# Three closing projections, the stages behind them and the end in halves of the tokens, with no barrier between

## The reference

```python
def second_block(x, ...):
    pos = jnp.arange(x.shape[1], dtype=jnp.int32)
    for layer in range(DEPTH):                                   # 2
        h = rmsnorm(x, norm_mix_pre[layer])
        if layer < N_A_LAYERS:
            m = retention_mixer(h, ...)                          # ends with 2048 -> 1024
        else:
            m = dilated_mixer(h, ..., k_sh, v_sh, pos)           # ends with 1024 -> 1024
        x = x + rmsnorm(m, norm_mix_post[layer])
        f = conv_ffn(rmsnorm(x, norm_ffn_pre[layer]), ...)       # ends with 2816 -> 1024
        x = x + rmsnorm(f, norm_ffn_post[layer])
        if layer == N_A_LAYERS - 1:
            k_sh, v_sh = shared_kv(x, kv_norm, att_w_kv, pos)
    return x

def rmsnorm(x, g):
    y = x * lax.rsqrt(jnp.mean(x * x, axis=-1, keepdims=True) + RMS_EPS)
    return y * g
```

## Time and profile before

| what | value |
|---|---|
| three runs | 2992.29, 2993.57, 2996.12 us |
| median | 2993.57 us |
| profiled execution, first to last instruction | 2993.2 us |
| instructions | 39031 |
| TensorE busy | 2953.5 us, 99% |
| TensorE weight loads | 2355.3 us, 79% |
| VectorE busy | 1719.4 us, 57% |
| ScalarE busy | 1049.0 us, 35% |
| GpSimd busy | 1279.0 us, 43% |
| mean granted clock of TensorE | 0.993 of 2.4 GHz |

### The profile page before, as it was taken

One profiled execution on the slowest core, in us unless ns is written; L12 is line 12 of the kernel. 1 busy time (PEld: TensorE's weight loads), 2 busy tenths in 40 slices (PEclk: granted clock), 3 DMA queues, 4 the chain that ended last, 5 costly groups with the idle time before them and its releaser, 6 DMA issues.

```text
span 2993.2 us, 39031 instructions
## 1 busy us (share of the span) xinstructions
PE 2953.5 (99%) x15224; PEld 2355.3 (79%) x15224; DVE 1719.4 (57%) x3004; ACT 1049.0 (35%) x1863; POOL 1279.0 (43%) x926
## 2 busy tenths in 40 slices
PE   8999999999999999999999999999999999999999
PEld 6777778887777778777778788887888888788887
DVE  4765455475745555735553587615766666587721
ACT  4443343354443432533322322224333333432221
POOL 3333334453333345544444455544434434355543
PEclk9999999999999999999999999999999999999999
DMA  5222223232222223232222233322222222223332
GB/s 194 81 78 67 71 78 96 85 113 71 78 64 71 78 85 99 85 106 78 85 85 79 83 99 95 98 96 95 78 78 71 78 78 78 71 88 96 99 99 71
DMA packets 78331, 260.22 MB, mean 87 GB/s; under 512 B 10730, under 2 KB 13546, under 8 KB 78148
## 3 DMA queue, kind: packets, MB, share of 16 engines
q1 hardware_dynamic: 77572, 255.63, 26.9%
q10 hardware_dynamic: 576, 2.10, 0.2%
HBM read 255.53 MB, written 6.09 MB: 87 GB/s over the span
## 4 chain that ended last, share of the span: by engine, by line
PE 93%; DVE 3%; ACT 1%; DMA 1%; issue 1%; POOL 0%; SPq 0%; PEldq 0%; DVEq 0%; ACTq 0%; PEld 0%
PE bank L707 25%; PE bank L709 24%; PE bank L708 24%; PE bank L845 2%; PE bank L892 2%; PE bank L872 1%; PE bank L724 1%; PE bank L1059 1%; PE bank L725 1%; PE bank L731 1%; PE bank L1009 1%; PE bank L1010 1%; PE bank L1015 1%; PE bank L1095 1%; PE bank L761 1%
## 5 line engine op out<-in xcount | busy, mean ns | idle before, releaser
L558 POOL TENSOR_TENSOR w_lo<-w_raw,w_hi 128x512 fp32r<-128x512 f32 x458 | 610.8, 1334 | 1630.9 <-ACT w_hi L1234 1630.9
L707 PE MATMUL bank<-h_hi,w_hi 128*128 128x512 f32 x2367 | 944.9, 399 | 0.5 <-POOL w_lo L558 0.5
L709 PE MATMUL bank<-h_hi,w_lo 128*128 128x512 f32 x2367 | 924.4, 391 | 0.0
L708 PE MATMUL bank<-h_lo,w_hi 128*128 128x512 f32 x2367 | 923.0, 390 | 0.0
L1234 ACT CAST w_hi<-w_raw 128x1024 fp32r<-128x1024 f32 x458 | 479.9, 1050 | 1259.4 <-PE bank L709 1164.2
L560 POOL TENSOR_TENSOR w_lo<-w_raw,w_hi 128x512 fp32r<-128x512 f32 x458 | 665.1, 1452 | 36.0
L707 PEld LDWEIGHTS bank<-h_hi,w_hi 128*128 128x128 f32 x2367 | 445.5, 188 | 97.4 <-issue 8.8
L709 PEld LDWEIGHTS bank<-h_hi,w_lo 128*128 128x128 f32 x2367 | 444.9, 188 | 95.8
L708 PEld LDWEIGHTS bank<-h_lo,w_hi 128*128 128x128 f32 x2367 | 446.1, 188 | 86.4 <-issue 0.3
L2107 DVE TENSOR_SCALAR m<-bank,gains 128x512 f32<-128x512 f32 x48 | 36.0, 751 | 328.6 <-ACT ta L1437 197.0
L1372 ACT ACTIVATE probs<-probs,small_columns 128x128 f32<-128x128 f32 (+2 forms) x192 | 101.9, 531 | 168.3 <-DVE small_columns L1866 164.1
(11 more groups left out here) (311 smaller groups left out, 4411.9 us busy)
## 6 DMA issues: line engine op xcount, KB each, us to landing
w_raw<-in_w SPq DMA_DIRECT2D x458, 512.0 KB, 3.5
bias_copies<-bias_vectors SPq DMA_DIRECT2D x1, 2560.0 KB
x_res<-in_x_t ACTq DMA_DIRECT2D x4, 512.0 KB, 8.3
bias<-bias_copies SPq DMA_DIRECT2D x8, 256.0 KB, 3.3
bias<-bias_copies SPq DMA_DIRECT2D x16, 128.0 KB, 2.4
out_x<-x_res SPq DMA_DIRECT2D x8, 256.0 KB, 2.9
bias_copies<-bias_vectors SPq DMA_DIRECT2D x1, 1280.0 KB
ple_raw<-in_p_t SPq DMA_DIRECT2D x2, 512.0 KB, 3.6
```

What stands on the lines that cost most here:

```text
L558: pool.tensor_tensor(WL[slot][:, 0:half], RAW[slot][:, 0:half], WH[slot][:, 0:half].bitcast(F32), ALU.subtract).then_inc(sems["lo_half"], 1)
L707: pe.matmul(banks[bank][:], WH[slot][:, w], hi[:, k, :], start=start, stop=False)
L708: pe.matmul(banks[bank][:], WH[slot][:, w], lo[:, k, :], start=False, stop=False)
L709: pe.matmul(banks[bank][:], WL[slot][:, w], hi[:, k, :], start=False, stop=stop).then_inc(sems["kt_done"], 1)
```

## The change

The last tile of `linear` in ret and ffn, and the last two in dil, are multiplied in two halves of 256 tokens: all steps for the first half, then all steps for the second half with the same weights, in another bank. Each half has its own sums, variance, root, reciprocal and two transposes. The next stages ffn0, dil, ffn1 and end have no barrier before them. Their first three tiles are multiplied in halves too: all k for half 0, then all k for half 1. DVE and ACT make x, `h_hi` and `h_lo` by halves, with separate operations. In dil the two operands change places (HH and H2H), and all eight `kv_hi` come behind both halves. At the end, half 0 is scaled, added and stored before half 1. The core of the diff, with new functions in full:

```diff
+HALF_ROW = SEQ // 2
+HALVES = (slice(0, HALF_ROW), slice(HALF_ROW, SEQ))
+IN_HALVES = {"post": 0, "ret": 1, "ffn": 1, "dil": 2}
...
 # SP
-            sp.wait_ge(sems["x_ready"], 4 * KT)
+            sp.wait_ge(sems["x_ready"], 6 * KT)
...
+            for k in range(KT):
+                sp.wait_ge(sems["x_ready"], 8 * KT + k + 1)
+                sp.dma_start(out[:, k, HALVES[0]], X[:, k, HALVES[0]]).then_inc(sems["stored"], t.add("stored", 16))
...
 # POOL
-            pool.wait_ge(sems["x_ready"], 4 * KT)
+            pool.wait_ge(sems["x_ready"], 6 * KT)
...
+        BEHIND_HALF = ("ffn0", "dil", "ffn1", "end")
...
-                if e.stage > 1 and name not in BEHIND_PLE:
+                if e.stage > 1 and name not in BEHIND_PLE and name not in BEHIND_HALF:
                     e.begin_stage()
...
 # PE
+                def half_tile(self, bank, hi, lo, k, start, stop, h, name=None):
+                    slot, w, c = self.n // SLOT % RING, slice(self.n % SLOT * P, (self.n % SLOT + 1) * P), HALVES[h]
+                    self.weights_in()
+                    pe.matmul(banks[bank][:, c], WH[slot][:, w], hi[:, k, c], start=start, stop=False)
+                    pe.matmul(banks[bank][:, c], WH[slot][:, w], lo[:, k, c], start=False, stop=False)
+                    ins = pe.matmul(banks[bank][:, c], WL[slot][:, w], hi[:, k, c], start=False, stop=stop)
...
+                def later_sums(self, name):
+                    split = IN_HALVES[name]
+                    t.up("m_squared", split)
+                    pe.wait_ge(sems["m_squared"], t.at("m_squared"))
+                    self.half_sums(name, [TC, TA, TB] if split == 2 else [TC, TB], 1, True, True).then_inc(sems["summed"], t.one("summed"))
+                def fresh_halves(self, opened, hi, lo, half, name):
...
+                    for h in range(2):
+                        self.n = base
+                        for k in range(KT):
...
+                            pe.wait_ge(sems["operand_hi"], t.at("operand_hi", behind))
...
+                            for bank in opened:
...
+                                pe.matmul(half(banks[bank][:], h), WH[slot][:, w], half(hi[:, k, :], h), start=(k == 0), stop=False)
+                                pe.matmul(half(banks[bank][:], h), WL[slot][:, w], half(hi[:, k, :], h), start=False, stop=False)
...
+                            pe.wait_ge(sems["operand"], t.at("operand", behind))
...
+                                ins = pe.matmul(half(banks[bank][:], h), WH[slot][:, w], half(lo[:, k, :], h), start=False, stop=(k == KT - 1))
+                                if h == 1:
+                                    ins.then_inc(sems["kt_done"], 1)
+                            if (h, k) == (0, 0):
+                                self.later_sums(name)
+                            elif (h, k) == (0, 3):
+                                self.half_spread(name, 1)
...
 # PE, linear
-                    for _ in range(first, KT):
+                    split = IN_HALVES[name]
+                    for _ in range(first, KT - split):
...
+                    if split:
+                        opened, n = [self.rotate() for _ in range(split)], self.n
+                        for bank in opened:
+                            for k in range(nk):
+                                self.half_tile(bank, hi, lo, k, k == 0, k == nk - 1, 0, "half_done" if k == nk - 1 else None)
+                        self.n = n
+                        pe.wait_ge(sems["evicted"], self.tiles - split)
+                        self.half_sums(name, [TC], 0, True, False)
+                        for at_ in range(split):
...
+                            for k in range(nk):
+                                self.half_tile(bank, hi, lo, k, k == 0, k == nk - 1, 1, "kt_done")
+                                if (at_, k) == (0, 0):
...
+                                    self.half_sums(name, [TA, TB] if split == 2 else [TB], 0, False, True).then_inc(sems["summed"], t.one("summed"))
+                                elif (at_, k) == (0, 4):
+                                    self.half_spread(name, 0)
+                        return
...
 # ACT
+                def operand_halves(self, name, dst, g, half_of_x, half, sq, squared):
+                    half_root(0)
+                    for h in range(2):
+                        for k in range(KT):
+                            t.up("x_ready")
+                            act.wait_ge(sems["x_ready"], t.at("x_ready"))
+                            act.activation(half(dst[:, k, :], h), half_of_x(X[:, k, :], h), ACT.Copy, scale=gain(g, k)).then_inc(sems["operand_hi"], t.one("operand_hi"))
+                            if h:
+                                act.activation(sq[:, k, :], X[:, k, :], ACT.Square).then_inc(sems[squared], t.one(squared))
+                            elif k == 0:
+                                hi(self.n - 2 * SLOT)
+                            elif k == 2:
+                                hi(self.n - SLOT)
+                            elif k == 4:
+                                self.squares(name, 1)
+                                hi(self.n)
+                            elif k == 6:
+                                half_root(1)
...
 # ACT, dilated
-                    self.postnorm(M2)
+                    self.operand_halves("ffn", HH, "mixpre1", by_class_half, in_class_half, SQD, "dil_squared")
                     for k in range(KT):
-                        t.up("x_ready")
-                        act.wait_ge(sems["x_ready"], t.at("x_ready"))
-                        act.activation(in_class(H2H[:, k, :]), by_class(X[:, k, :]), ACT.Copy, scale=gain("mixpre1", k)).then_inc(sems["operand_hi"], t.one("operand_hi"))
-                        act.activation(SQD[:, k, :], X[:, k, :], ACT.Square).then_inc(sems["dil_squared"], t.one("dil_squared"))
-                        for j in ((k // 2,) if k % 2 else ()) + (tuple(range(KT // 2, KT)) if k == KT - 1 else ()):
-                            act.activation(in_class(HH[:, j, :]), by_class(X[:, j, :]), ACT.Copy, scale=gain("kv", j)).then_inc(sems["kv_hi"], t.one("kv_hi"))
+                        act.activation(in_class(H2H[:, k, :]), by_class(X[:, k, :]), ACT.Copy, scale=gain("kv", k)).then_inc(sems["kv_hi"], t.one("kv_hi"))
                     t.up("cleared", 6)
                     self.past(3, KT)
...
 # DVE
+                def postnorm_halves(self, name, l, g, half_of_x, half):
...
+                    half_variance(name, 0)
+                    half_inverse(0)
+                    for h in range(2):
+                        t.up("rstd_spread")
+                        dve.wait_ge(sems["rstd_spread"], t.at("rstd_spread"))
+                        if h:
+                            dve.wait_ge(sems["evicted"], self.tiles)
+                        scaled(0, h)
+                        added(0, h)
+                        for k in range(KT):
+                            if k + 1 < KT:
+                                scaled(k + 1, h)
+                            dve.wait_ge(sems["x_ready"], t.at("x_ready"))
+                            t.up("operand_hi")
+                            dve.wait_ge(sems["operand_hi"], t.at("operand_hi"))
+                            dve.scalar_tensor_tensor(half(HL[:, k, :], h), half_of_x(X[:, k, :], h), gain(g, k),
+                                                     half(HH[:, k, :].bitcast(F32), h), ALU.mult, ALU.subtract).then_inc(sems["operand"], t.one("operand"))
+                            if k + 1 < KT:
+                                added(k + 1, h)
+                            if (h, k) == (0, 5):
+                                half_variance(name, 1)
+                        if h == 0:
+                            half_inverse(1)
+                            self.second_half(name, l)
```

More of the change, by code:

```diff
@@ new lines, in half_sums @@
+                def half_sums(self, name, squares, h, first, last):
+                    for a, sq in enumerate(squares):
+                        for b in (2 * h, 2 * h + 1):
+                            ins = pe.matmul(banks[sums_bank(name, h)][:, b:b + 1], sq[:, b * P:(b + 1) * P], ONES[:, 0:1],
+                                            start=(first and a == 0 and b == 2 * h),
+                                            stop=(last and a == len(squares) - 1 and b == 2 * h + 1), skip_group_check=True)
+                    return ins
@@ L967, in close @@
                         pe.wait_ge(sems["scaled"], t.at("scaled"))
-                        pe.matmul(banks[CLOSE_BANKS[k]][:], ID[:], M2[:, k, :], start=False, stop=True).then_inc(sems["added"], t.one("added"))
+                        pe.matmul(banks[CLOSE_BANKS[k]][:, c], ID[:], M2[:, k, c], start=False, stop=True).then_inc(sems["added"], t.one("added"))
                     self.tiles -= BY_PE
@@ L986, in ffn_up @@
                 def ffn_up(self, l):
-                    self.spread(OUTB)
```

(39 more changed lines are left out.)

155 lines of the change are left out of this document (103 added, 52 removed).

## The result

The changed kernel takes 3009.4 us (median of 4 runs, 3007.97 to 3010.22) against 2994.47 for the kernel before in the same comparison: 1.0047 of its time, 95% interval 1.0034 to 1.0059. Forecast were 3007.8 us and "slower" with 0.66. The profiled execution has a span of 3008.1 us, 14.9 more than before's 2993.2.

What follows compares the result with a forecast made beforehand. TensorE, busy 99% of 2993.2 us, was taken as the bound. Terms of -0.1 + 5.5 + 0.5 + 9.4 + 1.7 - 2.8 = +14.2 us gave 3007.8 us, range 2999.5 to 3019, down to 2993.5 for A.

Steps and rivals of the forecast that it cites:

- Step (1): Closing tiles and next stages' first tiles: a half matmul costs 0.120 us, or 0.113 if cost goes by column.
- Step (2): New stages' first tiles: the DVE and ACT cycle per half k takes 1.47 us, 1.91 in class order.
- Step (3): Next stages' starts, without POOL and clock: -0.1 us behind retention, +0.5 behind the dilated stage, +5.5 before kv.
- POOL terms: First-half chains: seven weight chunks, each lengthening DVE's operations by 1.34 us while POOL makes its low part.
- The kv order: Dilated stage's start: eight kv high parts, 9.0 us, precede the next weights' cast; TensorE waits over 3 us; loss 5.5.
- Step (4): First-half chains: POOL's low parts of seven chunks hold DVE for 9.4 us in all; bounds nothing and 15.4.
- Step (5): TensorE's cold clock after waits: hidden at the first k, 1.7 us lost before kv; bounds 0 and 10.
- Step (6): End of the kernel: the span ends 29.2 us after the last tile's start against 32.0, a gain of 2.8.
- A: First-half chains: half operations slip between POOL's, so no hold; 2996.7 us, no measurable change; chance 0.16.
- C: Before kv: a late TensorE hides the kv high parts, +5.5 us falls to 1, total 3003; within the chain's 0.66.
- B: Seams: TensorE sets the end and the halves hide the norm, -20.2 us, 2973.4 in all; chance 0.13.
- D: Chains: TensorE stays at 1.2 GHz, each chain lengthens by up to 7 us, 3021 or more; chance 0.05.

Runs made afterwards that it cites:

- e2: Changed kernel with DVE adding x two k ahead of the low part instead of one behind it: 2991.6 us, 0.9988 of the kernel before.
- e4: Changed kernel with the second half's sums behind the first half's k = 4, not 0, and spread behind k = 7, not 3: 3013.39 us, 1.0057.
- e3: Changed kernel with next weights cast behind the fourth kv high part, not the eighth, and three chunks loaded before SP waits for x: 3007.59 us, 1.0037.
- e9: e7 plus e3's cast and loads, and the kv reciprocal moved behind the last kv low part: 2988.05 us, 0.9974 of the kernel before.
- e7: e2 with the second half's sums behind the first half's k = 2 and its spread behind k = 7: 2990.62 us, 0.9983.
- e5: Changed kernel with GpSimd making only 64 of 1024 columns of seven chunks' low parts in the first-half chains: 3003.44 us, 1.0032.
- e6: Changed kernel with halves only in ffn 1's closing tile and the close, the other three seams as before: 2991.61 us, 0.9990.

## Why the prediction was right, step by step

**Step (1), half matmuls.** In the closing tiles they start 0.120 us apart (48 in 5.75 us), the price taken.

**Step (2), the half cycle.** 1.47 us forecast and 1.47 measured; 1.91 and 1.89 to 1.94 in class order. That this chain, and not TensorE, sets the end is shown by e2: with the wait for ACT out of the cycle it falls to 1.06 and each seam of this form shortens by 4.4 to 5.5 us, though the halves, their fixed cost and TensorE's work stay as they are.

**Step (3), the early start.** DVE's first scaling starts at S + 8.85 behind retention (9.0 forecast). N was S + 36.7, with two of the seven POOL terms of 1.34 S + 39.4; measured S + 40.4. The last `added` is at S + 36.3 where step (3) with POOL's part says 35.4: POOL's part is 0.7 longer than taken, and from the eighth `added` to the next half's first it is 3.0 us where 2.7 was counted, of which DVE stands 0.55 for the second spread. Behind the dilated stage 40.5 was forecast with POOL's part and 42.5 measured: POOL's part is 1.0 longer, and the stretch between the halves is 4.3 us. There TensorE sums squares of two tiles at half clock and the spread comes later. The prediction had the cold clock hidden at the first k; here it cost 1.0 to 1.2 us by this spread. e4 shows it by an edit, and e3, whose program is the same at this seam, by chance: its clock was low for a shorter time, the spread went out at S + 26.1 instead of 27.2, and N is 1.0 earlier. The stretches around the cold clock, first in the changed kernel, then in e3:

```profile
2624.40:2635.50 11.10, 8.35 (x39) 8.35 (x40) 8.18 (x16) 3.50 (x8) 3.92 (x3) 0.54 0.29 96
2623.40:2630.60 7.20, 5.50 (x26) 5.50 (x27) 5.79 (x11) 3.08 (x8) 2.88 (x3) 0.56 0.35 102
```

For kv, S + 54.4, with three POOL terms 58.4 and with the clock 60.1, against 57.7 measured to the start: the 1.7 us of clock were not lost there, and 3 x 1.34 was 0.6 too much.

**The kv order.** Eight kv high parts in a row take 9.03 us (9.0 forecast), and TensorE then waits 3.5 us on `w_lo`. e3 shows that the cast's place is the cause of the late start, and that moving the cast alone gains 0.75 us at the end of the kv matmuls. With the reciprocal moved as well it is 5.9 (e9 against e7), of which 2.5 are a clock that stayed up; the reciprocal was not moved alone.

**Step (4), POOL.** The mechanism was right, and the size nearly so. In the first half behind retention the two chunks lengthen the chain by 3.4 us (13.7 for 7 x 1.47 = 10.3), 1.7 each where 1.34 was taken; behind ffn 0 three chunks lengthen it by 3.4 (16.75 for 7 x 1.91), 1.1 each, and behind the dilated stage two by 3.7 (13.97). That makes 10.5 us on the chain, 9.4 forecast. e5 takes 10.0 of them away (3.3, 3.4 and 3.3), and the starts behind come 1.6, 3.4 and 3.8 us earlier, 8.8 in all; what is missing is DVE's wait for the second spread behind retention. That the marks gained only 5.6 is the clock's doing.

**Step (5), the clock.** Forecast 1.7 us, lost before kv. It was not lost there: the kv matmuls ran at 1.00 and took 11.0 us. Instead 1.7 us were lost behind N of retention, where TensorE's wait of 1.8 us for the first weights was followed by 3.4 us at a granted clock of 0.51 (1.2 GHz): from N to the sums it is 9.9 us for 8.2. Right size, wrong place, by luck: in e4 and e5 such stretches stand at two more places, 1.6 us each. And the cold clock at the first k, put at nothing, cost 1.0 to 1.2 us behind the dilated stage, as said under step (3).

**Step (6), the close.** The gain was 4.1 us, 2.8 forecast. DVE's last `added` starts at S + 24.4 and ends at 24.8, where 25.2 was forecast, and the end follows 3.1 us behind, for the 4.0 taken: the span ends at S + 27.9 instead of 29.2. e6 shows that the gain stands alone.

**The sum.** By seams: forecast +2.6, +3.2 and +11.2 us (retention, dilated, ffn 0 with the clock) and -2.8, measured +5.4, +5.1, +8.4 and -4.1. The total of 14.9 against 14.2 is closer than its terms: two were 2 to 3 us short, one 3 us long, and the close 1.3 short of its gain. The mechanism held, but that the sum fell within 1 us is luck.

**The rivals.** A, no hold by POOL, gave 2996.7; with the hold taken out (e5) the kernel is still at 3003.4. The starts are near step (3): N at S + 38.8 and 38.7 for 36.7 and 37.8, kv at 54.3 for 54.4. What A leaves out is the clock, some 5 us in e5 (1.8, 1.6 and 1.6), and the wait for the second spread behind retention. C, a kv order that hurts less, is out: without the hold the kv matmuls still start over 5 us later than before the change. B, halves that hide the norm, named 1.08 us as the cycle from which it decides. e2 and e7 reach 1.06. The sign then turns, to 0.9988 and 0.9983, but most of B's 5.5 us at a seam stays out: S to N behind retention is 35.0 us in e7, with a clock of 1.00 and TensorE busy for 32.0 of them, not 31.3. What is left is mainly TensorE's wait for the second half's first high part, 1.5, and one for the next weights, 1.2. D, a clock that stays down in the chain, is refuted: it is 1.00 in e4 over the whole chain.

## What to carry to other kernels

Halving a step's width halves neither DVE's nor ACT's part of it; before a producer chain that hands each tile from DVE to ACT and back is cut finer, work out its cycle with the waits in it and compare it with the consumer's, and give DVE one or two tiles of lead in its queue, which here was worth as much as the whole change cost. Where a stage is made to start earlier, look at what is cast, loaded or inverted in the same queues at that time: here the second spread, the kv reciprocal and the sums of the squares each became the next wait as soon as the one ahead of it was gone. Price each seam by itself, from its first matmul to a common mark; four seams of opposite sign hid behind one total.

## What the runs showed of the hardware that was not expected

After a wait of 1.8 to 3.5 us TensorE's granted clock did not always fall, and the length of the wait does not tell. Behind the wait of 1.8 us before N behind retention it was 0.51 (1.2 GHz) for 3.4 us. Behind a wait of 1.8 us before N behind the dilated stage it stayed at 1.00 in the same execution, and fell in e3, e4 and e5 (36 matmuls in 9.9 us for 8.3). The 48 kv matmuls behind a wait of 3.5 us ran at 1.00 in the changed kernel (11.0 us) and at 0.86 in e4 and e5 (12.6 us), and behind 3.0 us at 0.78 in e2 (13.9 us). What decides it is open. It is worth up to 3 us at a place, as much as several of the edits tried here.

Of DVE's operations of 256 columns only those with two operands in SBUF were held by GpSimd: `added` up to 1.52 us for 0.42 (e2), `h_lo` up to 1.12 for 0.48. The scaling, with an operand in PSUM, took 0.41 to 0.43 wholly beside GpSimd in e2. Not every operation with two operands in SBUF is held: the `added` of e2 that starts at 1677.58 lies wholly beside GpSimd's operation from 1677.43 to 1679.14 and took 0.42 us.
